# First stage of a three-block kernel: shift, scale and token mixes made tile by tile

## The reference, cut to what matters

```python
cond = jax.nn.silu(c)                                   # c: 1 x 1024
mod = cond @ ada_w[i] + ada_b[i]                        # 6 x 1024 outputs per block
sh1, sc1, gt1, sh2, sc2, gt2 = jnp.split(mod[:, None, :], 6, axis=-1)
hin = x * (1 + sc1) + sh1                               # 512 x 1024
...
h_prev = jnp.pad(h, ((0, 0), (1, 0), (0, 0)))[:, :-1]   # the token before
xx = h_prev - h
xs = h[None] + xx[None] * mu[:, None, None, :]          # six mixes: r, k, v, w, a, g
r, k, v = jnp.einsum('pbtd,pde->pbte', xs[:3], w_rkv)
w = -jax.nn.softplus(-(w0 + jnp.tanh(xw @ w1) @ w2)) - 0.5
a = jax.nn.sigmoid(a0 + (xa @ a1) @ a2)
g = jax.nn.sigmoid(xg @ g1) @ g2
```

## Time and profile before

| | |
|---|---|
| median of 3 runs | 2956.15 us (2953.92 to 2958.39) |
| profiled execution | 2953.57 us, span 2951.8 us |
| PE, busy share of the span | 94% |
| DVE | 46% |
| ACT | 34% |
| POOL | 8% |
| mean granted TensorE clock | 0.97 |
| moved by DMA | 261.05 MB, mean 88 GB/s |

### The profile page before, as it was taken

The page is one execution under the profiler, slowest core; times in us unless marked ns, Lnnn a source line. Parts: engine busy times, 40 slices in busy tenths (PEclk is TensorE's granted clock), DMA queues, the critical chain, the costliest instruction groups (busy, mean ns, idle before and its releaser), DMA issues.

```text
span 2951.8 us, 46143 instructions
## 1 busy us (share of the span) xinstructions
PE 2763.5 (94%) x18948; PEld 1993.5 (68%) x18948; DVE 1368.8 (46%) x2256; ACT 997.4 (34%) x1542; POOL 250.3 (8%) x218
## 2 busy tenths in 40 slices
PE   4999998889999899999999899999899898999999
PEld 1566666478888445678888688886555556788876
DVE  7666565253333276653333534433324756344335
ACT  1334333153422125544332423221111664333224
POOL 1232332010000004110000200000000100000000
PEclk9999999999999899999999899999789999999999
DMA  5234433222232110122232122222121002222212
GB/s 218 100 129 134 140 125 117 100 86 99 99 112 88 48 57 29 37 93 99 94 112 93 46 97 99 100 94 81 43 79 50 2 16 86 85 99 100 103 68 78
DMA packets 47010, 261.05 MB, mean 88 GB/s; under 512 B 5080, under 2 KB 7528, under 8 KB 28040
## 3 DMA queue, kind: packets, MB, share of 16 engines
q1 hardware_dynamic: 46280, 254.23, 24.6%
q10 hardware_dynamic: 576, 4.57, 0.4%
HBM read 256.63 MB, written 2.15 MB: 88 GB/s over the span
## 4 chain that ended last, share of the span: by engine, by line
PE 87%; DVE 5%; ACT 3%; DMA 1%; issue 1%; PEld 1%; POOL 1%; SPq 0%; DVEq 0%; ACTq 0%; PEldq 0%; POOLq 0%
PE psum L214 85%; PE psum L1888 2%; DMA weights<-in_ada 1%; PEld psum L214 1%; DVE residual L1378 0%; DVE weights L250 0%; POOL ysum L544 0%; DVE residual L1370 0%; POOL branch_in L546 0%; ACT L590 0%; POOL join L539 0%; DVE keys_rstd L2497 0%; DVE cmp_blocks L2511 0%; ACT ln_in L1333 0%; ACT nsa_probs L1924 0%
## 5 line engine op out<-in xcount | busy, mean ns | idle before, releaser
L1494 ACT ACTIVATE ffn_weights_hi<-weights 128x1024 fp32r<-128x1024 f32 (+1 forms) x120 | 137.4, 1147 | 480.0 <-PE psum L214 480.0
L214 PE MATMUL psum<-ffn_in_hi,ffn_weights_hi 128*128 128x512 f32 x704 | 278.0, 395 | 14.3 <-DVE ffn_weights_lo L1497 9.7
L214 PE MATMUL psum<-ff_in_hi,ff_weights_hi 128*128 128x512 f32 x704 | 276.6, 393 | 11.8 <-DVE ff_in_lo L1384 7.4
L1494 ACT ACTIVATE ff_weights_hi<-weights 128x1024 fp32r<-128x1024 f32 (+1 forms) x120 | 137.6, 1147 | 431.8 <-PE psum L214 431.8
L214 PE MATMUL psum<-ffn_in_lo,ffn_weights_hi 128*128 128x512 f32 x704 | 276.1, 392 | 0.0
L214 PE MATMUL psum<-ffn_in_hi,ffn_weights_lo 128*128 128x512 f32 x704 | 275.8, 392 | 0.0
L214 PE MATMUL psum<-ff_in_lo,ff_weights_hi 128*128 128x512 f32 x704 | 275.5, 391 | 0.0
L214 PE MATMUL psum<-ff_in_hi,ff_weights_lo 128*128 128x512 f32 x704 | 275.3, 391 | 0.0
L1497 DVE TENSOR_TENSOR ff_weights_lo<-weights,ff_weights_hi 128x1024 fp32r<-128x1024 f32 (+1 forms) x116 | 156.0, 1345 | 252.6 <-ACT ff_weights_hi L1494 252.6
L1497 DVE TENSOR_TENSOR ffn_weights_lo<-weights,ffn_weights_hi 128x1024 fp32r<-128x1024 f32 (+1 forms) x118 | 157.2, 1334 | 112.1 <-ACT ffn_weights_hi L1494 112.0
L214 PEld LDWEIGHTS psum<-ffn_in_hi,ffn_weights_hi 128*128 128x128 f32 x704 | 133.5, 190 | 46.2 <-DVE ffn_weights_lo L1497 11.0
(11 more groups left out here) (494 smaller groups left out, 4932.7 us busy)
## 6 DMA issues: line engine op xcount, KB each, us to landing
weights<-in_ada SPq DMA_DIRECT2D x96, 512.0 KB, 4.2
weights<-in_ff_in SPq DMA_DIRECT2D x44, 1024.0 KB, 4.7
weights<-in_ffn_in SPq DMA_DIRECT2D x44, 1024.0 KB, 4.7
weights<-in_ff_out SPq DMA_DIRECT2D x16, 1408.0 KB, 6.0
weights<-in_ffn_out SPq DMA_DIRECT2D x16, 1408.0 KB, 6.1
weights<-in_rwkv SPq DMA_DIRECT2D x8, 1152.0 KB, 6.0
weights<-in_fox_qkv SPq DMA_DIRECT2D x4, 1536.0 KB, 6.5
weights<-in_rwkv SPq DMA_DIRECT2D x8, 640.0 KB, 4.0
```

Of the source, the lines that this page charges most:

```text
L214: return nc.tensor.matmul(out, lhsT, rhs, start=start, stop=stop)
L1494: return nc.scalar.activation(sp_.hi[u][:, 0:width], slot[s][:, u * width:(u + 1) * width], ACT.Copy)
```

## The change

The two functions become one, and the work goes feature tile by feature tile.

- The matrices of the first shift and scale come as 8 tiles of 1 MB, each with the shift rows (as before) and beside them the weights of the scale laid out for PE. They go through a ring of four buffers. The first low-rank weights come in two halves between them. `x` comes in four quarters, and the constants table behind them.
- The shift of a tile is a DVE row product as before; the scale is 8 matrix products on PE with one moving column each (`cond` as columns), into two banks in turn.
- For each tile DVE makes the shift, the scale and two small tables, `(1 - mu) * shift` and `(1 - mu) * scale`, for the six mixes.
- A mix is now `hin_prev * mu + ((1 - mu) * scale) * x + (1 - mu) * shift`. ACT makes the part without the neighbour (`own`), DVE adds the other in place. POOL makes no difference any more.
- The order on PE is: scale of tile j, then low-rank products of tile j-1. On DVE: row product, shift, scale and tables of tile j, then the three mixes of tile j-1. ACT makes the own parts of `k` before the low-rank results, and those of `r` and `v` behind them.

```diff
+            def act(act):
+                act.dma_start(vec[:, :], d["vectors"][:, :]).then_inc(tables_in, 16)
+                for q in range(4):
+                    act.dma_start(x[:, 2 * q:2 * q + 2, :], d["x"][:, 2 * q:2 * q + 2, :]).then_inc(x_in[q], 16)
                 act.dma_start(ca[:, :], d["const_all"][:, :]).then_inc(tables_in, 16)
...
                 for j in range(KT):
+                    act.wait_ge(x_in[j // 2], 16)
+                    act.wait_ge(*dve_done(f"kept scale{j}"))
                     nc.scalar.activation(h[:, j, :], x[:, j, :], ACT.Identity, bias=mod(0, SH1, j),
                                          scale=mod(0, SC1, j)).then_inc(*act_done.step(f"hin{j}"))
+                    if j >= 2:
+                        act.wait_ge(*pe_done(f"lora{j - 2}"))
+                    for n, m in enumerate("wag"):
+                        own_part(m, j, tmp[:, n, j % 2, :])
+                for j in range(KT):
+                    own_part("k", j, xs["k"][:, j, :])
                 act.wait_ge(*pe_done(f"lora{KT - 1}"))
...
+                for m in "rv":
+                    for j in range(KT):
+                        own_part(m, j, xs[m][:, j, :])
...
             def pool(pool):
-                for j in range(KT):
-                    pool.wait_ge(*act_done(f"hin{j}"))
-                    nc.gpsimd.tensor_tensor(xx[:, j, :], hin[:, j, 0:T], h[:, j, :], ALU.subtract)...
...
             def dve(dve):
+                dve.wait_ge(tables_in, 32)
+                small(kept[:, ONE, :, :], mu, -1.0, 1.0, ALU.mult, ALU.add)...
+                for j in range(KT + 1):
+                    if j < KT:
+                        dve.wait_ge(ada_in[j % 4], j // 4 * 16 + 16)
+                        rows = ring[j % 4][:, 0:D]
+                        nc.vector.tensor_tensor_reduce(rows, rows, cond, ..., accum_out=inner[:, j:j + 1])...
+                        small(mod(0, SH1, j), inner[:, j:j + 1], vcol("ada_b", j), None, ALU.add)...
+                        dve.wait_ge(*pe_done(f"scale{j}"))
+                        small(mod(0, SC1, j), ps[:, 2 + j % 2, 0:1], vcol("ada_b", KT + j), 1.0, ALU.add, ALU.add)...
+                        dve.wait_ge(*dve_done(f"scale{j}"))
+                        small(kept[:, SHIFT, :, j], kept[:, ONE, :, j], mod(0, SH1, j), None, ALU.mult)...
+                        small(kept[:, SCALE, :, j], kept[:, ONE, :, j], mod(0, SC1, j), None, ALU.mult)...
+                    if j >= 1:
+                        for n, m in enumerate("wag"):
+                            mix(m, j - 1, tmp[:, n, (j - 1) % 2, :])
...
             def pe(pe):
+                for j in range(KT + 1):
+                    if j < KT:
+                        pe.wait_ge(ada_in[j % 4], j // 4 * 16 + 16)
+                        if j >= 2:
+                            pe.wait_ge(*dve_done(f"scale{j - 2}"))
+                        for k in range(KT):
+                            last = mm(ps[:, 2 + j % 2, 0:1], ring[j % 4][:, D + k * P:D + (k + 1) * P],
+                                      columns_of_cond[:, k:k + 1], k == 0, k == KT - 1)
+                    f = j - 1
+                    pe.wait_ge(*dve_done(f"a{f}"))
                     for n in range(2):
-                        mm(ps[n * HD:(n + 1) * HD, n, :], w[:, n * HD:(n + 1) * HD], tmp[:, n, j % 2, :], j == 0, j == KT - 1)
+                        mm(ps[n * HD:(n + 1) * HD, n, :], w[:, n * HD:(n + 1) * HD], tmp[:, n, f % 2, :], f == 0, f == KT - 1)
```

More of the change, by code:

```diff
@@ L229, in build @@
         tables_in = sem("tables_in")
-        x_in = sem("x_in")
+        x_in = [sem(f"x{q}_in") for q in range(4)]
         modulated = sem("modulated")
@@ L251, in inner_product @@
                                                   op1=ALU.add, accum_out=inner[:, j:j + 1])
[L253 to L259, removed]
-            def sp(sp):
[L262 to L266, removed]
+        MIX = ["r", "k", "v", "w", "a", "g"]
@@ new lines, in time_mix_inputs @@
+        def time_mix_inputs(scope, hin):
+            h = hin[:, :, 1:T + 1]
+            xs = {m: keep(f"mixed_{m}", [P, KT, T], scope) for m in "rkv"}
+            lora = {m: keep(f"lora_{m}", [P, T], scope) for m in ("w", "a", "g0", "g1")}
+            pe_done = steps("mix_pe", [n for j in range(KT + 1) for n in [f"scale{j}"] * (j < KT) + [f"lora{j - 1}"] * (j >= 1)])
+            act_done = steps("mix_act", ["rows", "columns"] + [f"{m}{j}" for j in range(KT) for m in ("hin", "own w", "own a", "own g")]
+                             + [f"own k{j}" for j in range(KT)] + ["w", "a", "g0", "g1"] + [f"own {m}{j}" for m in "rv" for j in range(KT)])
+            dve_done = steps("mix_dve", ["kept"] + [n for j in range(KT + 1) for n in [f"{m}{j}" for m in ("inner", "shift", "scale", "kept shift", "kept scale")
+                                                                                     if j < KT] + [f"{m}{j - 1}" for m in "wag" if j >= 1]]
+                             + [f"{m}{j}" for m in "krv" for j in range(KT)])
+            zeroed, first_column = sem("gate_rows_zeroed"), sem("first_column_zeroed")
+            rows_in, columns_in = sem("cond_rows_in"), sem("cond_columns_in")
+            ada_in = [sem(f"ada_first{n}_in") for n in range(4)]
+            lora_in = [sem(f"lora_first{n}_in") for n in range(2)]
+            kept = keep("mixed_part", [P, 3, 6, KT], scope)
+            with ExitStack() as own:
+                tmp = keep("mixed_low_rank", [P, 3, 2, T], own)
+                first = keep("lora_first", [P, KT * 288], own)
+                ring = [slot[s][:, 0:2 * D] for s in range(2)] + [keep(f"ada_first{n}", [P, 2 * D], own)[:, :] for n in range(2)]
+                columns_of_cond = keep("cond_columns", [P, KT], own)
+            ONE, SCALE, SHIFT = range(3)
+            mu = vec[:, VC["mu"][0]:VC["mu"][0] + 6 * KT].rearrange("p (m j) -> p m j", j=KT)
+            last_use[0], last_use[1] = (dve_done, f"w{KT - 3}", 0), (dve_done, f"w{KT - 2}", 0)
+            width = KT * 288 // 2
+            def sp(sp):
+                sp.dma_start(cond, d["c_rows"][:, :]).then_inc(rows_in, 16)
+                sp.dma_start(columns_of_cond[:, :], d["c_columns"][:, :]).then_inc(columns_in, 16)
+                for j in range(KT):
+                    if j >= 4:
+                        sp.wait_ge(*dve_done(f"inner{j - 4}"))
+                        sp.wait_ge(*pe_done(f"scale{j - 4}"))
+                    sp.dma_start(ring[j % 4], d["ada_first"][j, :, :]).then_inc(ada_in[j % 4], 16)
+                    if j in (0, 2):
+                        half = slice(j // 2 * width, (j // 2 + 1) * width)
+                        sp.dma_start(first[:, half], d["lora1"][0, :, half]).then_inc(lora_in[j // 2], 16)
@@ L276, in dve @@
[L276 to L319, removed]
@@ new lines, in act, with own_part @@
+                act.wait_ge(rows_in, 16)
+                nc.scalar.activation(cond, cond, ACT.Silu).then_inc(*act_done.step("rows"))
+                act.wait_ge(columns_in, 16)
+                nc.scalar.activation(columns_of_cond[:, :], columns_of_cond[:, :], ACT.Silu).then_inc(*act_done.step("columns"))
+                def own_part(m, j, out):
+                    n = MIX.index(m)
+                    nc.scalar.activation(out, x[:, j, :], ACT.Identity, bias=kept[:, SHIFT, n, j:j + 1],
+                                         scale=kept[:, SCALE, n, j:j + 1]).then_inc(*act_done.step(f"own {m}{j}"))
@@ L320, in act @@
                 for j in range(KT):
+                    act.wait_ge(x_in[j // 2], 16)
+                    act.wait_ge(*dve_done(f"kept scale{j}"))
                     nc.scalar.activation(h[:, j, :], x[:, j, :], ACT.Identity, bias=mod(0, SH1, j),
-                                                    scale=mod(0, SC1, j)).then_inc(*act_done.step(f"hin{j}"))
+                                         scale=mod(0, SC1, j)).then_inc(*act_done.step(f"hin{j}"))
+                    if j >= 2:
+                        act.wait_ge(*pe_done(f"lora{j - 2}"))
@@ L328, in act @@
                 nc.scalar.activation(lora["g1"][0:32, :], ps[0:32, 7, :], ACT.Sigmoid).then_inc(*act_done.step("g1"))
+                for m in "rv":
+                    for j in range(KT):
+                        own_part(m, j, xs[m][:, j, :])
             def pool(pool):
-                pool_done.enter(pool)
+                nc.gpsimd.memset(hin[:, :, 0:1], 0.0).then_inc(first_column, 1)
                 nc.gpsimd.memset(lora["g1"][:, :], 0.0).then_inc(zeroed, 1)
-                nc.gpsimd.memset(hin[:, :, 0:1], 0.0).then_inc(*pool_done.step("zero"))
@@ L343, in dve @@
             def dve(dve):
                 dve_done.enter(dve)
[L345 to L352, removed]
+                small = nc.vector.tensor_scalar
+                dve.wait_ge(tables_in, 32)
@@ L3136 @@
     d["vectors"] = np.concatenate(vectors, 1)
-    d["ada"] = np.concatenate([a["ada_w"][i].T.reshape(6 * KT, P, D) for i in range(2)])
```

(5 more changed lines are left out.)

67 lines of the change are left out of this document (39 added, 28 removed).

## The result

| | before | changed |
|---|---|---|
| median, 4 runs each | 2956.31 us | 2985.68 us (2985.64 to 2993.48) |
| ratio | | 1.0105, 95% interval 1.0093 to 1.0118 |
| profiled execution | 2953.57 us, span 2951.8 | 2985.70 us, span 2983.9 |
| POOL busy | 250.3 us | 239.6 us |
| ACT busy | 997.4 us | 1031.8 us |

The forecast was 2985 us (2964 to 3002) and slower. The time is decided by a few moments, and these are read from the timelines.

What follows compares the result with a forecast made beforehand. PE bounds the kernel, busy 94% but idle during this stage. Low-rank products ending 20.2 us later, r's start 6.7 and its slow beginning 2.1 sum to 29.0 us, giving 2985 us (range 2964 to 3002).

Steps and rivals of the forecast that it cites:

- Start: Beginning of the stage: DVE starts at about 14, tile 1 lands about 16, PE's first low-rank products at 21.7 us.
- A turn: Loop over feature tiles: low-rank products 5.2, scale 1.8, tables, mixes and hand-overs 2.25; 9.25 us from tile to tile.
- all low: Pricing of the loop with PE always at the lower clock level: products 6.1 us a tile, 11.75 us a turn.
- Last two tiles: End of the loop: two tiles of low-rank products back to back without a scale, 2 x 5.2 us, ending at 87.6.
- Behind the products: Between low-rank products and r: ACT's 16 own parts make r start 16.8 us behind (+6.7); r's slow start adds 2.1.
- Sum: Whole kernel: 20.2 + 6.7 + 2.1 = 29.0 us slower, giving a median of 2985 us, +1.0%.
- A (full clock): Rival in the loop: the clock does not fall, turn 7.05 us; 11.5 us slower in all, 2968; chance 0.20.
- B (all low): Rival in the loop: PE never becomes quick within a tile; 45.8 us slower in all, 3002; chance 0.12.
- C (no loop): Rival: scale products slip in beside low-rank ones, DVE sets 4.2 us a tile; sum -5.6 us, 2951; chance 0.10.
- D (the part behind costs nothing): Rival ahead of r: r's start isn't what is late, so 20.2 us slower, 2976; chance within the forecast's 0.58.

Runs made afterwards that it cites:

- the table ahead: Changed kernel with the constants table issued on ACT's queue ahead of the four quarters of x; 2987.12 us, 1.0103 of the kernel before.
- gap-filled run: Changed kernel with two unread 128x512 products added on PE behind each scale but the first; 2975.83 us, 1.0061 of the kernel before.
- own parts early: Changed kernel with ACT making the own parts of k, r and v in each tile's turn; 2979.85 us, 1.0080 of the kernel before.
- scale on DVE: Changed kernel with the scale made as a second DVE row product, none on PE; 2962.91 us, 1.0019 of the kernel before.
- scale ahead: Changed kernel with PE making the scale of tile j+2 ahead of tile j's low-rank products; 2961.85 us, 1.0021 of the kernel before.
- three repairs: Changed kernel with PE's scale two tiles ahead, constants table ahead of x, all own parts in each tile's turn; 2951.05 us, 0.9975 of the kernel before.

## Why the prediction was right, step by step

- **Start.** First low-rank products at 26.0, forecast 21.7. The step that failed is "The bytes of this queue are the same, so DVE starts at about 14": SP's queue has rows of 8 KB and ACT's now of 4 KB, and ACT now has six transfers to issue where it had three. DVE is 6.4 us late, the first products 4.3: with the table ahead they came at 22.5, so DVE's start is 3.5 of it, and 0.8 is tile 1, there at 16.8 in that run for the 16.0 of the forecast. The slow first scales were as forecast, 3.5 us.
- **A turn.** The order (low-rank products, scale, tables, two mixes, hand-over) is what the trace has. Mean of the six turns 9.48 (26.02 to 82.91), forecast 9.25. The parts: products 4.6 to 5.8 (mean 5.4) where 5.2 was taken, scale 1.95 to 2.23 where 1.8 was. Each tile starts low and becomes quick on its way, as forecast, but later than in the first tile of before: three of the six took 5.8, which is nearly the 6.1 of all low, and two took 4.9 and 4.6. That their mean is near 5.2 is in part luck; in the run with the table ahead, the same loop, it was 5.5. The gap-filled run gives the same turn at full clock, 7.09 for 7.05. The forecast counted 4.1 us of the turn as "one column or nothing"; PE's idle time alone was 2.1 of 9.5 us, and the clock fell in each turn all the same.
- **Last two tiles.** 8.3 us, forecast 10.4: they come back to back and the second ran at full clock. With the start and the turns this gives 4.3 + 1.4 - 2.1 = 3.6 us, the distance between 87.6 and 91.3.
- **Behind the products.** `r` 16.64 us behind, forecast 16.8; `r` longer by 1.8, forecast 2.1. Both confirmed by moving ACT's own parts.
- **Sum.** 29.0 us forecast, 32.1 in the profiled executions, 29.4 in the medians. The exact hit of the median is luck: the profiled executions stand 2.7 us below (before) and at (changed) their medians.
- **Rivals.** A (full clock) is what the gap-filled run shows; it didn't occur by itself. B (all low) neither: the scale behind each tile's products took 1.95 to 2.23 us, so the quick level was reached by the end of each tile, if late. C (no loop) needed another order, and with it the turn was 4.92, under the 5.1 named as the point of decision; the kernel was then still slower by 0.21%: its products start at 26.9 where that sum has 21.7, and `r` is 18.3 us behind the end, not 16.8. D (the part behind costs nothing) fell with the own parts early.
- **What the forecast left out.** That ACT would have the own parts of `k` on its hands when the products end early; `r` stood 1.0 to 1.7 us further behind the end in three experiments for it, in the changed kernel not at all.

## What to carry to other kernels

When two engines with fixed orders feed each other within one step, write down the turn (each wait, and what stands ahead of the producer in its own order) before judging by busy shares; one tile more of look-ahead took 27 us off this stage. Put short follow-up work of a critical engine ahead of bulk work that nobody waits for yet, or into its idle turns. And price bursts of products with waits between them at both levels of the clock.

## What the runs showed of the hardware

- Bursts of products with one moving column ran at the slow rate from end to end: 16 records took 3.54 us from 10.8 and 3.57 from 17.2, 0.22 each, and 1.95 when they followed low-rank products. The profile writes the granted clock as 1.00 at 10 to 20, so before its first fall the durations have to be read, not that column.
- A tile's low-rank products take 3.11 us at full clock, 4.6 to 5.8 behind 4 us of one-column products and waiting, and unread products in the wait bring back 3.11 at a granted clock of 1.00. An idle time of 2.0 us in a turn of 5.1 us was enough for 4.7 (scale on DVE), and with PE busy without a break, 1.95 us of one-column products in each 4.92 us, the clock still fell once (4.7 in scale ahead, 4.5 in the three repairs).
- Two DMA queues at full load shared by the size of their rows, with nearly as many packets on each: a third of the bytes with rows of 4 KB beside 8 KB, two thirds with 16 KB beside 8 KB; 12.9 against 16.6 us to landing for the same table behind the same bytes.
- The rest of the span from `r` on, one execution each, varied from 2873.8 to 2882.8 us between kernels that have the same instructions there, and single executions of one kernel spread by up to 12 us. A change of a few microseconds at the start needs many runs.
